# Last layer's attention by query, masks in one pass, and the first modulation in pieces, in a four-layer float32 kernel

## The chip, the cores and the metric

One core of one Trainium2 chip runs the whole program. The metric is the device time of one execution in microseconds; before the change it is 2213.15 (median of 3 runs, 2212.28 to 2214.16). Engines are named as in the profile: PE (TensorE, matrix products), DVE (VectorE), ACT (ScalarE), POOL (GpSimd), SP (SyncE, which issues most transfers).

## The reference

Two blocks of two layers each work on one sequence x of 256 tokens by 1024 features beside a context of 256 tokens. All is float32.

- Each layer: a modulation (six vectors of 1024, from a condition vector times a 1024 x 6144 matrix, for x and for the context), a norm scaled and shifted by it, an input projection, a mixer, an output projection, a second norm and a gated feed-forward of 2816 hidden features.
- Layers 0 and 1 mix by a bidirectional mLSTM, a spatial gating unit and a convolution. Layer 2 mixes by attention, half of its heads with a window of 128 around the query, masked by -1e30. Layer 3, the last, is differential attention, only for the 256 tokens of x:

```
s = einsum('bqhad,bkhad->bhaqk', q, k) * scale        # 8 heads, a = 0, 1, d = 64, 512 keys
p = softmax(s, axis=-1)
a = p[:, :, 0] - lam * p[:, :, 1]
o = einsum('bhqk,bkhe->bqhe', a, v)                    # e = 128
out = (rms(o) * subln * (1 - lam_init)) @ w_out
```

Queries and keys are normed over their 64 features and rotated before that.

## The kernel before

**Layout.** Features lie on partitions, tokens in columns: x and the context together are 512 columns (X and C, 256 each), 8 tiles of 128 features. Every weight product is made of three one-pass products (float32r): high times high, high times low, low times high (`mm3`). The high and low parts of each weight item (1024 rows by 256 columns, 1 MB) are made on the way: ACT rounds (`high_weights`, L2229), DVE subtracts (`low_weights`, L1459), in two halves. Items come through a ring of four slots (`weights` in `sync_program`), SP issues them in order. Attention's own products (scores, logits, sums, transposes) are plain f32.

**Order.** Each engine has its program written out in order, and semaphores (`Signal`) join them. An instruction waits for its counts and all behind it on its engine wait too.

**The start.** SP loads the first third of layer 0's modulation (columns 0 to 2047, shift and scale) as eight steps of 128 rows by 2048 columns into two slots, each step waiting for the product two before it. PE multiplies each with the condition vectors (`mod_step`, 4 products of 512 columns, 32 rows of output each), ACT copies the rows out, PE turns them to columns (`mod_turn`), DVE adds the bias (`bias`) and makes the gains. Only then does `normed` (DVE scales, ACT adds the shift and rounds, DVE makes the low part) feed `first_tiles`: four tiles, products in order of the features as they come (`FIRST`). Meanwhile DVE squares x and the context, POOL adds the squares, PE averages them, ACT makes the root.

**Layer 2's masks.** Windowed scores and logits get their mask as one more product, the identity times `window`, both f32: 16 of 128 columns (`even_scores`) and 8 of 256 (`even_logits`).

**Layer 3.** `odd_projection` makes 24 tiles: per pair of heads two key tiles, two query tiles (256 columns), two value tiles (`ODD_TILES`). Keys and queries are squared by ACT, averaged over heads by PE (`odd_head_sums`), made to roots by ACT, scaled and rotated by DVE (`odd_scaled`, `odd_rotated`, with `odd_swap` on PE). Between tiles PE makes score pairs by query (`odd_scores`: 128 queries, 512 keys, both maps, into banks 2 and 3), and DVE takes only their maxima. After the last tile `odd_mixer` runs 20 steps. Per step, half a head: PE makes the logits anew by key (`odd_logits`, with the maxima subtracted by two products from turned rows), ACT makes the exponentials, PE multiplies both maps with the values (`odd_product`, 512 columns), DVE adds exponentials for the sums of the softmax (`odd_chunks_added`), PE sums them over partitions (`odd_sum`). Per head ACT makes the reciprocal, DVE scales and joins the maps (`odd_joined`), ACT squares, PE averages (`sub_mean`). After every four heads `sub_norm` makes the factors with a square root (another table set of ACT) and a reciprocal. `upper_mixed` multiplies the first four heads' features with the first two output items while the last four wait for their factors; `mixer_out` goes on with the lower features.

Of the kernel before, what the change touches and what calls it, by code (L numbers as in the profile page):

```python
# [13 lines left out]
P = 128  # L14
D = 1024
# [58 lines left out]

THIRD = 2048
SIDES = 2
# [44 lines left out]
class Plan:  # L121
# [54 lines left out]
    def schedule(self):  # L176
# [14 lines left out]
        for s, (place, g) in enumerate(places):  # L191
            self.mod_steps.setdefault(place, []).append(s)
            if s + SIDES < len(places) and s + SIDES >= KD:
                before = g + 6 if g >= 0 else 2
# [8 lines left out]
    def memory(self):  # L203
# [26 lines left out]
        self.decay = sb("state_decay", P, 2, TC, HEADS)  # L230
        self.carried_m, self.minus_end_m = sb("carried_maximum", 64, 5), sb("minus_maximum_at_end", 64, 4)
# [7 lines left out]
        self.odd_rows = at("odd_shift_rows", [P, 4, SEQ], F32R, offset=room)  # L239
# [22 lines left out]
        self.h_low = at("input_low", [P, KD, TOK], F32R, offset=scr_at + (2048 + KD * TOK) * 4)  # L262
        self.bank = [nc.alloc_psum_tensor(f"bank{b}", [P, 512], F32) for b in range(8)]
# [39 lines left out]
        self.od_o, = self.cut(0, (8, SEQ))  # L303
        self.od_PT = big[:, 16:22, :].rearrange("p (b a) n -> p b a n", b=3)
        self.od_rec = big[:, 22, :]
        self.od_pre = [big[:, 23, :], self.rs[:, :]]
        self.sub_sq, self.od_shift = big[:, 0:2, C], big[:, 2, C].rearrange("p (b r) -> p b r", b=2)
        self.sub_ok, self.sub_ms = big[:, 3, C], big[:, 4, C]
        self.od_max, self.od_least = (big[:, 5, SEQ + 8 * q:SEQ + 8 * q + 8].rearrange("p (b j) -> p b j", b=2) for q in range(2))
# [31 lines left out]
    def mod_rows(self, third):  # L341

        return self.scr[:, 0:TOK] if third == 0 else self.rs[:, :]
# [9 lines left out]
    def out_bank(self, L, e):  # L353

        return self.bank[(0, 1, 3, 4)[e % 4] if L == 3 else e % 4]

# [42 lines left out]
    def signals(self):  # L399
        nc = self.nc  # L400

        def S(name, *parts):
# [9 lines left out]
        self.tables_again = S("tables_loaded_again", (0, 7 * 16), (2, 2 * 16))  # L412
        self.stored = nc.alloc_semaphore("stored")
# [4 lines left out]
        self.consts, self.conditions = S("constants_set", (0, 8)), S("conditions_activated", (0, 4))  # L418
        self.params_v, self.lam_exp = S("parameters_derived", (0, 9)), S("lambda_exponents", (0, 2))

        self.stepped, self.mod_out, self.mod_turned = S("modulation_steps_multiplied", (0, 96)), S("modulation_rows_out", (0, 12)), S(
            "modulation_turned", (0, 12))
        self.biased, self.gains = S("modulation_thirds_biased", *((l, 3) for l in layers)), S(
            "norm_gains_made", (0, 4), (1, 4), (2, 5), (3, 4))
# [4 lines left out]
        self.first_squared = S("first_squares_made", *((p, KD) for p in halves))  # L429
        self.squared = S("squares_made", *((p, KD * kinds[p]) for p in order))  # L430
# [58 lines left out]
        self.keys_spread, self.even_set = S("keys_spread", (2, 4)), S("even_constants_set", (0, 4))  # L489
# [8 lines left out]
        self.odd_scores, self.odd_max = S("odd_score_pairs", (0, 16)), S("odd_maxima", (0, 32))  # L498
        self.odd_set, self.odd_shift, self.odd_turned = S("odd_constants_set", (0, 4)), S("odd_shifts", (0, 8)), S("odd_shifts_turned", (0, 4))
        self.odd_high, self.odd_low = S("odd_shifts_high", (0, 4)), S("odd_shifts_low", (0, 8))  # L500
# [2433 lines left out]
```

## Time and profile before

| | |
|---|---|
| runs | 2212.28, 2213.15, 2214.16 us |
| profiled execution | 2211.64 us, span 2209.9 us |
| PE busy | 2106.5 us (95%) |
| DVE busy | 1319.5 us (60%) |
| ACT busy | 996.1 us (45%) |
| POOL busy | 415.4 us (19%) |
| granted PE clock, mean | 0.99 |

The span is the stretch of the profiled execution in which engines work; the execution's own time is 1.7 us longer. PE is the busiest engine; its matmuls are pipelined, so a row's duration holds a latency, and the distance from one start to the next is what an instruction costs in a run of them.

### The profile page before, as it was taken

To read this page: it belongs to the slowest core of one execution; us is meant where nothing else is said; L and a number is where in the kernel's file an instruction comes from. 1 tells how busy PE (TensorE), PEld (TensorE's weight loads), DVE (VectorE), ACT (ScalarE), POOL (GpSimd) and SP (SyncE) were. 2 spreads that over 40 slices of the span, in tenths; PEclk is the share of its full clock that TensorE was granted. 3 is DMA by queue.
4 is the path that set the end of the run, shared out by engine and by line. 5 is a ranking of instruction groups with operands and counts; after the bars stand their busy time and mean duration, and the time that the engine had idled before them with its cause. 6 is when DMAs were issued, how large, how long until landed. Compare 5 with 4: busy or idle time off the path is not lost.

```text
span 2209.9 us, 32689 instructions
## 1 busy us (share of the span) xinstructions
PE 2106.5 (95%) x13156; PEld 1693.0 (77%) x13156; DVE 1319.5 (60%) x2156; ACT 996.1 (45%) x1756; POOL 415.4 (19%) x308
## 2 busy tenths in 40 slices
PE   5999799999999899999999999999999999989999
PEld 2766677978987786999965447797898777648999
DVE  5293757945963666655554345794596555556555
ACT  2434744523542646544553353452354343355443
POOL 1000416502521003000100231650352100000000
PEclk8999999999999999999999999999999999999999
DMA  9654023563466336456533002346344322103563
GB/s 348 205 203 140 20 77 112 185 206 128 172 222 218 120 95 209 135 172 203 179 127 141 1 1 96 132 164 200 109 164 160 126 77 78 56 15 118 170 214 115
DMA packets 264534, 310.07 MB, mean 140 GB/s; under 512 B 5568, under 2 KB 251456, under 8 KB 252096
## 3 DMA queue, kind: packets, MB, share of 16 engines
q1 hardware_dynamic: 259680, 303.33, 41.2%
q10 hardware_dynamic: 4704, 4.65, 0.6%
q8 instruction: 105, 1.72, 0.3%
q14 instruction: 45, 0.37, 0.1%
HBM read 306.91 MB, written 1.05 MB: 139 GB/s over the span
## 4 chain that ended last, share of the span: by engine, by line
PE 80%; DVE 8%; ACT 6%; issue 2%; DMA 2%; POOL 1%; SPq 0%; ACTq 0%; DVEq 0%; POOLq 0%
PE bank L687 79%; DVE weights_low L1465 2%; ACT weights_high L2237 1%; DMA modulation_slots<-w_mod 1%; DVE scratch L1457 1%; DVE big L1457 1%; DVE yT L1457 1%; PE bank L696 1%; DVE big L1953 0%; DVE input_low L1457 0%; DMA modulation_slots<-mod_w 0%; DVE big L2070 0%; DVE token_sums L1813 0%; DVE xT L1457 0%; POOL weight_slots L596 0%
## 5 line engine op out<-in xcount | busy, mean ns | idle before, releaser
L687 PE MATMUL bank<-input_high,weights_high 128*128 128x256 f32 (+1 forms) x2336 | 750.7, 323 | 16.1 <-DVE weights_low L1465 5.4
L687 PE MATMUL bank<-input_high,weights_low 128*128 128x256 f32 (+1 forms) x2336 | 736.2, 317 | 0.0
L687 PE MATMUL bank<-input_low,weights_high 128*128 128x256 f32 (+1 forms) x2336 | 715.0, 317 | 5.7 <-DVE input_low L1457 5.2
L1465 DVE TENSOR_TENSOR weights_low<-weight_slots,weights_high 128x1024 fp32r<-128x1024 f32 (+2 forms) x344 | 391.8, 1178 | 215.4 <-ACT weights_high L2237 214.6
L687 PEld LDWEIGHTS bank<-input_high,weights_high 128*128 128x128 f32 x2336 | 440.4, 189 | 91.8 <-issue 41.2
L687 PEld LDWEIGHTS bank<-input_low,weights_high 128*128 128x128 f32 x2336 | 434.1, 189 | 43.7 <-DVE input_low L1457 10.2
L687 PEld LDWEIGHTS bank<-input_high,weights_low 128*128 128x128 f32 x2336 | 440.2, 188 | 33.7
L2237 ACT ACTIVATE weights_high<-weight_slots 128x1024 fp32r<-128x1024 f32 (+2 forms) x348 | 314.2, 950 | 160.9 <-PE bank L687 147.9
L1808 DVE TENSOR_TENSOR weights_low<-weight_slots,weights_high 128x512 fp32r<-128x512 f32 x216 | 232.0, 1092 | 28.2 <-ACT weights_high L2503 26.1
L687 PE MATMUL bank<-hidden_high,weights_high 128*128 128x256 f32 (+1 forms) x704 | 240.4, 341 | 0.5 <-DVE weights_low L1465 0.4
L687 PE MATMUL bank<-hidden_low,weights_high 128*128 128x256 f32 (+1 forms) x704 | 237.8, 338 | 0.0
L687 PE MATMUL bank<-hidden_high,weights_low 128*128 128x256 f32 (+1 forms) x704 | 237.7, 338 | 0.0
L658 POOL TENSOR_TENSOR yT<-yT 128x256 f32<-128x256 f32 (+1 forms) x66 | 63.4, 965 | 691.4 <-ACT yT L2259 559.1
L1457 DVE SCALAR_TENSOR_TENSOR xT<-bank,modulation,xT 128x256 f32<-128x256 f32 x144 | 64.4, 479 | 208.0 <-PE bank L687 208.0
L687 PEld LDWEIGHTS bank<-hidden_high,weights_high 128*128 128x128 f32 x704 | 132.5, 188 | 30.7 <-issue 8.4
L687 PEld LDWEIGHTS bank<-hidden_high,weights_low 128*128 128x128 f32 x704 | 132.4, 188 | 16.3
L687 PEld LDWEIGHTS bank<-hidden_low,weights_high 128*128 128x128 f32 x704 | 132.5, 188 | 15.4
L2503 ACT ACTIVATE weights_high<-weight_slots 128x512 fp32r<-128x512 f32 x216 | 129.0, 622 | 29.2 <-PE bank L687 14.5
L687 PE MATMUL bank<-modulation_slots,condition_vectors 128*32 128x512 f32 x768 | 103.3, 630 | 25.3 <-DMA modulation_slots<-w_mod 15.6
L687 PE MATMUL bank<-token_sums,weights_high 128*128 128x256 f32 x576 | 105.0, 280 | 3.8 <-ACT scratch L2550 2.6
L687 PE MATMUL bank<-big 64*128 64x256 f32 (+2 forms) x352 | 96.0, 483 | 6.1 <-DVE big L1953 3.0
L591 POOL TENSOR_TENSOR weight_sum<-weight_slots 128x512 f32<-128x512 f32 x36 | 49.2, 1367 | 251.3 <-DVE weights_low L1808 142.7
(284 smaller groups left out, 2678.4 us busy)
## 6 DMA issues: line engine op xcount, KB each, us to landing
modulation_slots<-w_mod SPq DMA_DIRECT2D x48, 1024.0 KB, 7.2
modulation_slots<-mod_w SPq DMA_DIRECT2D x48, 1024.0 KB, 6.7
weight_slots<-w_gu SPq DMA_DIRECT2D x44, 1024.0 KB, 5.1
weight_slots<-ffn_w_in SPq DMA_DIRECT2D x44, 1024.0 KB, 5.1
weight_slots<-w_in SPq DMA_DIRECT2D x24, 1024.0 KB, 5.3
weight_slots<-w_down SPq DMA_DIRECT2D x16, 768.0 KB, 4.8
weight_slots<-ffn_w_out SPq DMA_DIRECT2D x16, 768.0 KB, 4.9
weight_slots<-od_w_in SPq DMA_DIRECT2D x12, 1024.0 KB, 5.1
```

Source lines behind the costliest of these rows:

```text
L591: pool.tensor_tensor(m.weight_sum[:, :, :], a21, a22, ALU.add).then_inc(m.weights_added.sem, 1)
L658: pool.tensor_tensor(o, yT[:, 2 + q, t] if k == 1 else o, yT[:, 2 + i % 4, t], ALU.add).then_inc(m.square_joined.sem, 1)
L687: return pe.matmul(o, w, r, start=start, stop=stop, skip_group_check=shared)
L696: return pe.transpose(o, a, ident[0:a.shape[0], 0:a.shape[0]])
L1457: return stt(out=o, in0=a, scalar=s, in1=b, op0=op0, op1=op1)
L1465: tt(m.w_low[:, g % 2, c], m.ring[:, g % SLOTS, c], m.w_high[:, g % 2, c].bitcast(F32), ALU.subtract).then_inc(m.low_made.sem, 1)
L1808: tt(low, m.raw(run, j), high.bitcast(F32), ALU.subtract).then_inc(m.low_made.sem, 1)
L2237: F(m.w_high[:, g % 2, c], m.ring[:, g % SLOTS, c], ACT.Copy).then_inc(m.high_made.sem, 1)
L2503: F(m.split(j)[0], m.raw(run, j), ACT.Copy).then_inc(m.high_made.sem, 1)
```

## The change

Layer 3:
- The tiles come in another order, keys and queries ahead of values.
- Each of 16 steps x (a head, 128 queries) takes its exponentials from the very scores that gave the maxima: DVE's maxima, times -scale, are ACT's bias; ACT's exponential also sums over the 512 keys. DVE makes both reciprocals, the second times minus lambda; ACT scales the second map (`odd_second`), DVE scales the first and adds (`odd_mix`). PE transposes the joined map in four parts (`odd_flip`), ACT copies it out (`odd_keys`), and one product per head of four 256-column matmuls gives the output (`odd_product`).
- Of these steps 15 start between the projection tiles (`SCORES`, `FLIPS`, `PRODUCTS` give the tile behind which each comes). Logits, picks, turned shifts, the added exponentials and the sums by PE are gone. Head sums use one bank, value tiles two buffers.

Layer 2: the mask and the identity beside it are first copied to float32r, and their products are one-pass.

Start: the first third is loaded as eight pieces of 1024 rows by 256 columns, shift and scale of one pair of feature tiles after the other, into slots of their own. Four are multiplied before the projection, four between its first products. Each pair is copied out, turned, biased and made to gains by itself. The context's squares move from DVE to ACT.

```diff
-ODD_TILES = tuple(8 * part + 2 * i + t for i in range(4) for part in (1, 0, 2) for t in range(2))
+ODD_TILES = tuple(8 * part + 2 * i + t for part, i in ((1, 0), (0, 0), (1, 1), (0, 1), (2, 0), (1, 2), (0, 2), (2, 1), (1, 3), (0, 3), (2, 2), (2, 3)) for t in range(2))
+SCORES = {6: 0, 7: 1, 8: 2, 9: 3, 10: 4, 11: 5, 12: 6, 13: 7, 16: 8, 17: 9, 18: 10, 19: 11, 21: 12, 22: 13, 23: 14, 24: 15}
+FLIPS = {e + 2: x for e, x in SCORES.items()}
+PRODUCTS = {11: 0, 12: 1, 17: 2, 18: 3, 23: 4, 24: 5, 25: 6, 27: 7}
+FIRST_LOADED = tuple((j, k) for k in range(KD - 2) for j in range(2)) + ((0, KD - 2), (0, KD - 1), (1, KD - 2), (1, KD - 1))
+LOADING = {1: ((4,), ()), 2: ((5, 6), ()), 3: ((7,), (2,)), 4: ((), (3,))}
...
@@ sync_program @@
+        if third == 0:
+            at = D * (s % 2) + 256 * (s // 2)
+            sp.dma_start(m.piece(s), w[:, at:at + 256].rearrange("(k p) c -> p k c", p=P)).then_inc(m.loaded(s)[0], 16)
+            return
...
-    for s in range(SIDES):
+    for s in range(4):
         step(s)
     weights(0)
-    for s in range(SIDES, KD):
+    weights(1)
+    for s in range(4, KD):
         step(s)
-    weights(1)
+    weights(2)
...
@@ tensor_program, start @@
+    def first_piece(s):
+
+        i, what = divmod(s, 2)
+        pe.wait_ge(*m.loaded(s))
...
+        for k in range(KD):
+            j = k % 4
+            o = mm(bank[4 + i % 2][32 * j:32 * j + 32, 256 * what:256 * what + 256], m.cvec[:, k, :], m.piece(s)[:, k, :], k < 4, k >= 4)
+        o.then_inc(m.stepped.sem, 1)
+
+    def first_turn(i):
+        pe.wait_ge(*m.mod_out.at(0, i))
+        for c in range(4):
+            o = mm(bank[4 + i % 2][:, 2 * c:2 * c + 2], m.pair_rows(i)[:, c * P:(c + 1) * P], m.summed, True, True)
...
+    pe.wait_ge(*m.consts.at(0, 7))
+    for s in range(3):
+        first_piece(s)
+    pe.wait_ge(*m.columns_in.end(0))
     pe.wait_ge(*m.consts.end(0))
-    for k in range(KD):
-        mod_step(k)
-        if k in (4, 6):
-            add_squares(("first", k // 2 - 2), (X, C)[k // 2 - 2], m.first_squared)
-    pe.wait_ge(*m.columns_in.end(0))
-    mod_turn(0)
+    first_turn(0)
+    first_piece(3)
+    add_squares(("first", 0), X, m.first_squared)
+    add_squares(("first", 1), C)
+    first_turn(1)
     keep_busy(6, 8)
...
@@ tensor_program, layer 2 @@
-                i = mm(bank[2 + half][:, at:at + P], ident[:, :], m.window[:, kind, :], False, True, shared=True)
+                i = mm(bank[2 + half][:, at:at + P], m.unit[:, :], m.mask[:, kind, :], False, True, shared=True)
...
@@ tensor_program, layer 3 @@
+    def odd_flip(x):
+
+        pe.wait_ge(*m.odd_mixed.at(0, x))
+        if x:
+            pe.wait_ge(*m.odd_keyed.at(0, x - 1))
+        for k in range(TC):
+            o = turn(bank[6][:, k * P:(k + 1) * P], m.od_P[:, x % 3, 0, k * P:(k + 1) * P])
+        o.then_inc(m.odd_flipped.sem, 1)
+
+    def odd_product(h):
+        pe.wait_ge(*m.v_tokens.at(3, h | 1 if h < 4 else h))
+        pe.wait_ge(*m.odd_keyed.at(0, 2 * h + 1))
...
+        for k in range(TC):
+            o = mm(m.head_out(h).rearrange("p (c q) -> p c q", c=2), m.od_v[:, h, k, :], m.od_AT[:, h % 2, k, :, :], k == 0, k == TC - 1)
+        o.then_inc(m.odd_prod.sem, 1)
...
         if x:
-            pe.wait_ge(*m.odd_max.at(0, 2 * x - 1))
-        if x and x % 4 == 0:
-            pe.wait_ge(*m.odd_low.at(0, 2 * (x // 4) - 1))
+            pe.wait_ge(*m.odd_exp.at(0, 2 * x - 1))
...
+    def odd_step(e):
+
+        if e in SCORES:
+            odd_scores(SCORES[e])
+        if e in PRODUCTS:
+            odd_product(PRODUCTS[e])
+        if e in FLIPS:
+            odd_flip(FLIPS[e])
...
     def odd_mixer(L):
         odd_projection(L)
         pe.wait_ge(*m.projected.end(L))
         odd_tokens(7)
...
+        odd_step(24)
+        odd_step(25)
+        for u in range(2):
+            sub_spread(u)
+        odd_step(26)
+        for h in (4, 5):
+            sub_mean(h)
+        upper_mixed(L, 0)
+        odd_step(27)
+        sub_mean(6)
+        upper_mixed(L, 1)
+        sub_mean(7)
+        pe.wait_ge(*m.odd_keyed.end(0))
         for u in (2, 3):
             sub_spread(u)
...
@@ vector_program, layer 3 @@
     def odd_maximum(x):
...
+        if x >= 2:
+            dve.wait_ge(*m.odd_exp.at(0, 2 * x - 3))
+        dve.wait_ge(*m.odd_max.at(0, 2 * x + 1))
+        ts(m.od_least[:, x % 2, :], m.od_max[:, x % 2, :], -SCALE, None, ALU.mult).then_inc(m.odd_shift.sem, 1)
...
+    def odd_mix(x):
+        first, second = (m.od_P[:, x % 3, a, :] for a in range(2))
+        dve.wait_ge(*m.odd_second.at(0, x))
+        muladd(first, first, m.od_rec[:, x % 2, 0:1], second).then_inc(m.odd_mixed.sem, 1)
...
+        odd_mix(14)
         to_tokens(L, 7, m.od_v[:, 7, :, :], 4)
...
+        odd_step(24)
+        odd_reciprocals(15)
+        sub_norm(0, range(1, 2))
+        odd_mix(15)
+        odd_step(25)
+        sub_bounded(4)
+        for u in range(2):
+            odd_normalised(u)
+        odd_step(26)
+        sub_bounded(5)
+        next_weights(m.outp[L][0])
...
@@ scalar_program, layer 3 @@
+    def odd_exponential(x):
+
+        act.wait_ge(*m.odd_shift.at(0, x))
...
+        for a in range(2):
+            F(m.od_P[:, x % 3, a, :], bank[2 + a][:, :], ACT.Exp, bias=m.od_least[:, x % 2, a:a + 1], scale=SCALE,
+              accum_out=m.od_den[:, x % 2, a:a + 1]).then_inc(m.odd_exp.sem, 1)
+
+    def odd_second(x):
+        second = m.od_P[:, x % 3, 1, :]
+        act.wait_ge(*m.odd_rec.at(0, 2 * x + 1))
+        F(second, second, ACT.Identity, scale=m.od_rec[:, x % 2, 1:2]).then_inc(m.odd_second.sem, 1)
+
+    def odd_step(e):
+        if e in FLIPS:
+            odd_keys(FLIPS[e])
+        if e in SCORES:
+            odd_exponential(SCORES[e])
+            odd_second(SCORES[e])
...
@@ scalar_program, start @@
     ln_exp_tables()
+    pair_out(0)
+    act.wait_ge(m.inputs_in[1], 16)
+    for k in range(KD):
+        square(("first", 1), k, C)
+    pair_out(1)
+    high_weights(0)
     act.wait_ge(*m.square_added.end(("first", 0)))
     act.wait_ge(*m.square_added.end(("first", 1)))
     rstd("first", slice(0, TOK))
-    high_weights(0)
-    modulate("start", KD - 1)
```

## Rows read from the trace of the kernel before

**Rows 1.** The page, busy us (share) by engine, and the chain that ended last.

```profile
PE 2106.5 (95%) x13156; PEld 1693.0 (77%) x13156; DVE 1319.5 (60%) x2156; ACT 996.1 (45%) x1756; POOL 415.4 (19%) x308
...
PE 80%; DVE 8%; ACT 6%; issue 2%; DMA 2%; POOL 1%; SPq 0%; ACTq 0%; DVEq 0%; POOLq 0%
```

**Rows 2.** Windows of the last layer: stretch, busy us by engine, PEclk, DMA share, GB/s.

```profile
1771.00:1911.00 140.00, 135.41 (x653) 100.74 (x653) 73.50 (x125) 56.99 (x96) 0.00 (x0) 1.00 0.26 83
1911.00:1981.00 70.00, 69.68 (x293) 33.04 (x290) 40.46 (x75) 33.83 (x63) 0.00 (x0) 1.00 0.00 1
1981.00:1987.00 6.00, 0.03 (x1) 0.00 (x0) 3.73 (x5) 3.35 (x6) 0.00 (x0) 0.70 0.11 19
1987.00:1990.00 3.00, 2.93 (x11) 2.12 (x12) 1.33 (x5) 1.41 (x2) 0.00 (x0) 0.50 0.92 316
```

**Rows 3.** Timeline of the start: start us, us, engine, line, operation, [idle before].

```profile
22.48 5.43 DVE L2204 TENSOR_TENSOR yT<-xT 128x256 f32<-128x256 f32 x8 [2.94 <-DMA xT<-p_ctx]
...
35.11 0.69 ACT L2284 ACTIVATE rstd<-bank,eps 128x512 f32<-128x512 f32 x1 [22.99 <-PE bank L687]
...
36.69 1.06 PE L687 MATMUL bank<-modulation_slots,condition_vectors 128*32 128x512 f32 x8 [1.67 <-DMA modulation_slots<-w_mod]
...
38.98 1.03 PE L687 MATMUL bank<-ident,scratch 128*128 128x8 f32 x8 [1.23 <-ACT scratch L2252]
...
42.36 0.76 PE L687 MATMUL bank<-input_high,weights_high 128*128 128x512 f32 x1
...
66.14 0.39 PE L687 MATMUL bank<-input_high,weights_high 128*128 128x512 f32 x1
...
66.37 0.40 PE L687 MATMUL bank<-input_low,weights_high 128*128 128x512 f32 x1
```

**Rows 4.** One window of the start, columns as in group 2.

```profile
50.00:55.00 5.00, 5.00 (x23) 3.99 (x22) 5.00 (x14) 3.31 (x7) 0.00 (x0) 1.00 1.10 349
```

**Rows 5.** DMA issues of the first 60 us: KB each, median us to landing.

```profile
xT<-p_x ACTq DMA_DIRECT2D x1, 1024.0 KB, 12.9
```

**Rows 6.** Groups of instructions: out<-in, forms, count, busy us, mean ns.

```profile
L687 PE MATMUL bank<-tables,ident 128*128 128x128 f32 (+1 forms) x48 | 10.5, 343 | 0.0
```

**Rows 7.** Timeline between two projection tiles of the last layer.

```profile
1806.52 1.02 PE L687 MATMUL bank<-scratch,mean_over_head_halves 128*128 128x512 f32 x2
...
1807.21 2.00 ACT L2237 ACTIVATE weights_high<-weight_slots 128x1024 fp32r<-128x1024 f32 x2
...
1811.00 0.75 DVE L1457 SCALAR_TENSOR_TENSOR big<-big,parameter_columns,scratch 128x512 f32<-128x512 f32 x1 [7.23 <-ACT scratch L2728]
...
1811.67 1.28 DVE L2070 TENSOR_REDUCE big<-bank 128x1 f32<-128x512 f32 x2
...
1812.87 2.35 DVE L1465 TENSOR_TENSOR weights_low<-weight_slots,weights_high 128x1024 fp32r<-128x1024 f32 x2
...
1813.00 1.13 PE L687 MATMUL bank<-big 64*128 64x512 f32 x4
```

**Rows 8.** Timeline of the last layer's attention, from tile 23 to the output projection.

```profile
1910.84 0.60 PE L696 MATMUL bank<-ident,big 128*128 128x128 f32 x4
...
1913.45 1.14 PE L687 MATMUL bank<-big 64*128 64x256 f32 x8
...
1914.86 1.08 ACT L2757 ACTIVATE big<-bank 128x512 f32<-128x512 f32 x2 [3.22 <-PE bank L687]
...
1918.22 1.98 PE L687 MATMUL bank<-big,yT 128*128 128x512 f32 x4
...
1986.70 1.28 ACT L2775 ACT_TABLE_LOAD   x1
...
1987.07 1.06 PE L687 MATMUL bank<-big,mean_over_d 128*32 128x256 f32 x2 [6.04 <-DVE big L2112]
...
1989.73 1.75 DVE L2126 RECIPROCAL big<-big 128x256 f32<-128x256 f32 x1 [0.48 <-ACT big L2775]
...
1997.35 0.36 PE L687 MATMUL bank<-input_high,weights_high 128*128 128x256 f32 x1 [0.71 <-DVE input_low L2138]
```

More of the change, by code:

```diff
@@ L739, in keep_busy, with loading, first_tiles @@
             mm(bank[b][:, 0:P], m.mean_d[:, :], ident[:, :], True, True)
-    def first_tiles(items, n, place, part, last):
-        for j, k in FIRST:
+    def loading(k):
+        pieces, turns = LOADING.get(k, ((), ()))
+        for s in pieces:
+            first_piece(s)
+        for i in turns:
+            first_turn(i)
+    def first_tiles(items, n, place, part, last, first=False):
+        for j, k in FIRST_LOADED if first else FIRST:
+            if first and j == 0:
+                loading(k)
             if k in (0, KD // 2):
@@ L1373, in odd_projection @@
         odd_head_sums(1)
-        pe.wait_ge(*m.odd_set.end(0))
         for e in range(4, 24):
@@ L1486, in modulate, with first_pair @@
             bias(m.mod_turn[place])
+    def first_pair(i):
+        r = slice(2 * i, 2 * i + 2)
+        dve.wait_ge(*m.mod_turned.at(0, i))
+        o = m.mods[:, 0, :, 0:16].rearrange("p v (s k) -> p s k v", s=2)[:, :, r, :]
+        b = cols[:, L_TAB[0], B_MOD:B_MOD + 16].rearrange("p (s k) -> p s k", s=2)[:, :, r].unsqueeze(3).to_broadcast([P, 2, 2, 2])
+        tt(o, bank[4 + i % 2][:, 0:8].rearrange("p (s k v) -> p s k v", s=2, k=2), b, ALU.add).then_inc(m.biased.sem, 1)
+        dve.wait_ge(*m.biased.at(0, i))
+        for v in range(2):
+            muladd(m.coef[:, 0, v, r], m.mods[:, 0, v, 8 + 2 * i:10 + 2 * i], 1.0, column(L_TAB[0], N1 + 2 * i, 2), ALU.add,
+                   ALU.mult).then_inc(m.gains.sem, 1)
     def gains(l4, which):
         at, s = ((N1, 8), (N2, 32))[which]
-        dve.wait_ge(*m.biased.at(l4, 2 * which))
+        dve.wait_ge(*m.biased.at(0, m.third_at(3 * l4 + 2 * which)))
         for v in range(2):
@@ L1511, in normed @@
             t = slice(v * SEQ, (v + 1) * SEQ)
+            if L == 0 and which == 0 and i % (2 * per) == 0:
+                if k >= 2:
+                    for j in range(made, i):
+                        low(j)
+                    made = i
+                    first_pair(k // 2)
+                dve.wait_ge(*m.gains.at(0, k + 1))
             if k >= 2:
@@ L2297, in normed @@
             t = slice(v * SEQ, (v + 1) * SEQ)
+            if L == 0 and which == 0 and i == 4 * per:
+                pair_out(2)
+                pair_out(3)
             act.wait_ge(*m.norm_t.at(part, i))
@@ L2737, in odd_projection @@
             n = SEQ if tile < 8 else TOK
-            projected_tile(L, e, ACT.Copy, big[:, tile, 0:n], n, banks=2)
+            if tile >= 18:
+                act.wait_ge(*m.v_turned.at(L, tile - 18))
+            projected_tile(L, e, ACT.Copy, big[:, tile if tile < 16 else 16 + tile % 2, 0:n], n, banks=2)
             coming_weights(L, e)
```

446 lines of the change are left out of this document (187 added, 259 removed).

## The prediction

> **What bounds the kernel now.** The page comes first: PE is busy 95% of the span, and the chain that ended last is 80% PE, 8% DVE, 6% ACT [rows 1]. A change therefore gains where it takes PE work away or closes one of PE's few gaps. The windows of the last layer come next [rows 2]: while its tiles are projected (1771 to 1911) PE is busy 135.4 of 140 us at full clock, DVE only 73.5 and ACT 57.0; in the attention that follows (1911 to 1981) PE is busy 69.7 of 70, DVE 40.5 and ACT 33.8; then PE stands still for 6 us, and after it the granted clock is 0.50 (1.2 GHz). So PE is the limit of the attention and has no room; DVE and ACT have some 65 and 80 us of room under the projections. The start is another matter: there transfers and a chain of small steps hold the first projection back to 42.36 [rows 3, 4].
>
> **The last layer, PE work.** From the transposes after the next to last tile's products (1910.84, about the end of tile 23) to the first product of the output projection's lower half (1997.35) the kernel takes 86.5 us [rows 8]. PE's f32 costs: 512 columns over 128 rows take 0.43 each of two instructions, 0.85 a product (head sum, 1.02 with its latency [rows 7]); four instructions of 512 take 1.7 (1.98 with latency, [rows 8]); the pair of scores on 64 rows each 0.96 (1.13 with latency, [rows 7]); four transposes 0.5 (0.60). Gone are 16 logits (eight instructions of 256 columns, 0.8 [rows 8], and two picks, 0.5: 21 us), 16 halves of products (1.7 each: 27), 8 sums (0.85: 7), 4 turns of shifts (0.65: 3): 58 us. New are 16 flips (0.5: 8) and 8 products of four 256-column matmuls, 8 instructions at 0.21 (1.7: 14): 22 us. The 16 score pairs stay and now carry the exponentials. PE work falls by 36 us, but much of the rest moves under the projections, and PE is full there.
> Until tile 23 is done PE now has two more score pairs (14 instead of 12: 1.9), 12 flips (6), four products (6.8), four sub-norm sums (2), less three turns (2): +14.7.
>
> **The last layer, the new loop.** Each scored step now chains both other engines. From a tile's end ACT copies it out (0.5), in every second step cuts weights (2.0), squares (0.5) and makes the root (1.35); DVE scales (0.7) and begins the maxima 5.15 us after the tile's end (1806.52 to 1811.67 [rows 7]), and ends them at 6.4. New behind them: shift 0.2, a gap 0.2, two exponentials 1.3 (1.08 as now [rows 8], and 0.1 each for reading their sums), at 8.1; then reciprocal, product with lambda and the second map's scaling 1.5 (the scaling is a 128x512 pass of ACT like an exponential, about 0.6; two small DVE steps and gaps are the rest), at 9.6. Only then is ACT free for the next tile. In even steps DVE first mixes the last maps (0.7, as the scaling of that size, 0.75), then splits weights (2.35), scales and takes maxima: 8.2 to 8.9 from one exponential to the next. PE in the same time has its tile (24 matmuls at 0.233 [rows 3] or, for the 256 columns of queries, half of it: 5.6 or 2.8), head sum, swap, scores, flip and in some steps a product: 7.5 to 8.1 in key and value steps, but 4.7 to 7.4 in query steps. PE's next scores wait for the last exponentials (they share the banks). Going through the steps in order, the waits are 1.1 and 1.2 at scores 1 and 2, 1.3 and 2.1 at 6 and 7, 0.8 and 2.1 at 10 and 11, 0.5 at 12 (queries late in rotation); value steps without scores let the loop catch up. Sum 9.1. Waits of today in that stretch, for maxima and shifts, go: 3.8 of the 4.6 us idle. Queued behind ACT's long step are the copies out, which free PE's two banks; a copy late by up to 2 us is still ahead of the tile after the next. Tile 23 thus ends 14.7 + 9.1 - 3.8 = 20.0 later. Bounds: no waits at all, +11; every step at the loop's length with nothing caught up, +32.
>
> **The last layer, the tail.** Count from the end of tile 23. Scores 14 at 0.5, exponentials to 4.6, scores 15 to 5.7, product 5, flip 13, product 6, flip 14 to 10.9. DVE meanwhile mixes map 14, copies the last values and takes maxima 15 (to 9.4), ACT's exponentials end at 11.2, its scaling at 12.7; then a table load 1.28, the root, and DVE's reciprocal 1.75 [rows 8]: factors at 16.8. PE idles 6 us, spreads, flips map 15 (mixed only behind the factors) and idles 3.7 more until the first four heads are scaled, cut and head 5's squares are summed (24.1). Upper output tiles of 24 matmuls (2.8) to 26.9; product 7 to 28.6; copy, square, bound, and the second upper tiles beside them to 31.9; the last sum to 32.4. Now comes the end chain with nothing beside it: bounds, root, reciprocal, factor 4.0, spread, scale and cut 2.7 (today's chain from 1987.07 holds the same steps around its 24 + 24 upper products [rows 8]): 39.2. After each of the three long gaps I expect half clock for about 3 us as in the window from 1987 [rows 2], 4 us in all: 43.2. Against 86.5 that is -43.3. Together: 20.0 - 43.3 = **-23.3**, range -34 to -8.
>
> Today's rows have transposes four at a time between long products, at full clock [rows 2, 8]; the change adds 64. The Trainium skill (TensorE: Matmul & The Clock Gate, Part 4: PE-mode transpose) says that transposes don't count as busy for the clock as other matmuls do, which speaks against them. By the rows they cost 8 us in all and the sum stands; by that rule the clock could fall around them, which is rival 3.
>
> **The masks of the layer before.** The 24 window masks are f32 products with the identity, 48 instructions, 10.5 us busy [rows 6]. As one-pass products they are 24 instructions of at most the 0.117 that a one-pass product of 256 columns takes: 2.8. They stand in chains of PE itself (scores, maxima, next scores; logits, exponentials), so most of the 7.7 us shows: I take **-6**, range -7.7 to -3. Two small DVE copies (under 0.5 us) are issued before its first weights, where today two picks of 1.4 us in all cost nothing.
>
> **The start.** Today ctx lands at 22.5, the last of eight modulation transfers shortly before 36.69, each held by two slots; root, weights, turn (1.03), gains and first scaling bring the first product to 42.36; the 96 products of the first four tiles (22.4 at 0.233, as 66.14 to 66.37, and 1.4 for the second weights and half clock) end at 66.14 [rows 3]. The new order needs four of the eight pieces, x, ctx and two weights before it begins: 1.05 MB each, 8.9 MB with the small tables; in 1 KB rows the engines move 350 GB/s (349 in the window from 50, when the weights' 1 KB rows are under way [rows 4]). From 2.4 us that is 28, with weights 0 there at about 25. ACT's cuts (2.0), the root (1.3), first scaling and high part (1.5) give a start at 30.5. But then PE carries four pieces (1.06 each [rows 3]) and two turns (1.0 each) inside: 22.4 + 6.3 = 28.7, and 2.3 for the second weights and the low clock: 61.5, which is **-4.6**. The later pieces land at 31, 34, 37, 40, each a little ahead of its place; DVE's three pair steps (0.7 each) fit, since DVE needs 4.8 us for two k and PE 5.6 and more. Bounds: start at 28 and nothing late, -8.5; ctx late (below), +2.
> What sets ctx: x needed 12.9 us for 1 MB beside modulation rows of 8 KB [rows 5], and ctx came at 22.5 [rows 3]. If the queues share as today, it comes at 24 to 26, and its squares on ACT (8 of about 0.5) end at 28 to 30; that is the +2. The Trainium skill (DMA: Bandwidth & Descriptors, Queues, rings and completion order) says that each engine alternates between queues packet by packet; with 1 KB rows on both sides ctx would then come sooner, near 15. The sum would stay as it is, since weights 0 set the start then, and the worse end would fall away; the row of x agrees so far that the queue with the small rows got a quarter of the bytes.
>
> **Sum.** -23.3 - 6 - 4.6 = -33.9. The profiled execution took 2211.64 (span 2209.9), the runs' median is 2213.15, 1.5 more. 2211.64 - 33.9 = 2177.7, and with the 1.5: **2179 us**.
>
> **Rivals.**
> (1) The loop binds more than I count (a wait of mine is missing, as the single bank for head sums, or copies out late enough to hold tiles): every scored step at the loop's length, +12 in the projections: 2191. For it: 8.7 us loops against 4.7 us steps; against: the value steps give slack back.
> (2) The loop binds less and the tail overlaps better (clock not falling in it): -9: 2170. For it: DVE and ACT have 65 and 80 us of room [rows 2].
> (3) Slower: the clock. If waits of 1 to 2 us in each step, with flips between, let the granted clock fall to 0.50 under the projections, PE's some 150 us of work there double where it is low. The gain is gone once 34 us of this work run at half clock; with half of the 150 low it is 2179 + 75 = 2254. Against it: waits of up to 1.4 us in the kernel before left the clock at 1.00 over 140 us [rows 2].
> (4) The part at the start gives nothing or costs 2, since ctx and the turns come late: 2184 to 2186, within the forecast's range.
>
> **Chances.** Forecast with (4) (2171 to 2189) 0.58; (1) 0.17; (2) 0.12; (3) 0.07; something between that eats up most of the gain 0.06, half of it within 0.2% of before (about what can be told from no change). Faster 0.89, same 0.03, slower 0.08. The range of 8 in 10 reaches into (1) and (2): 2162 to 2206.
>
> **What would show it.** First product of the kernel at 29 to 33 and tile 4 at 60 to 63; fewer than 3 us of mask products; no logits, no picks; PE waits for exponentials at scores 1, 2, 6, 7, 10 and 11 of 1 to 2 us; tile 23 about 20 us later from the layer's start and its tail 39 to 47 us long, with two gaps of over 3 us and one before the last spreads. Wrong would be: a granted clock under 1.00 in the projections, waits of over 15 us there, a tail over 55 us, or a first tile group that ends no sooner than today.

## The result: 17 us faster, half of what was forecast

| | median of runs, us | lowest to highest | against before |
|---|---|---|---|
| before | 2213.53 | 2212.28 to 2214.16 (4) | 1 |
| after | 2195.82 | 2194.65 to 2200.44 (4) | 0.9923 [0.9911, 0.9936] |

The change makes the kernel faster by 0.77%. The forecast was 2179 with a range of 2162 to 2206: the time lies in the range, the gain (17.7 by the medians, 17.0 by the ratio) is half of the 34 forecast. The profiled executions took 2211.64 and 2194.65, 16.99 apart, and that difference can be divided. From the page of after, the two lines that [rows 1] shows of before:

```profile
PE 2079.4 (95%) x13092; PEld 1694.3 (77%) x13092; DVE 1306.3 (60%) x2173; ACT 1014.0 (46%) x1811; POOL 414.4 (19%) x308
...
PE 78%; DVE 9%; ACT 7%; issue 3%; DMA 1%; POOL 1%; ACTq 0%; SPq 0%; DVEq 0%; POOLq 0%
```

PE is busy 27.1 us less, and only 17 come out: 10 went into idle time. To find the places I took four instructions that stand in both kernels and set their starts beside each other: the first product of layer 2 (1105.72 before, 1101.69 after), the first product of layer 3 (1756.10, 1752.96), the transposes behind tile 23 (1910.84, 1931.76) and the first lower-half output product (1997.35, 1980.33). The stretch from layer 3's first product to the end of tile 23 is called the loop below, the one from there to the lower-half product the tail.

| stretch | before | after | difference | forecast |
|---|---|---|---|---|
| start to layer 2 | 1105.7 | 1101.7 | -4.0 | -4.6 |
| layer 2 to layer 3 | 650.4 | 651.3 | +0.9 | -6 |
| layer 3 to the end of tile 23 | 154.7 | 178.8 | +24.1 | +20.0 |
| tail | 86.5 | 48.6 | -37.9 | -43.3 |
| rest of the span | 212.6 | 212.7 | +0.1 | 0 |

The start did what was forecast. Of after, the timeline at the context's squares, at the first product and at the fifth tile (before's are in [rows 3]):

```profile
19.36 1.34 ACT L2314 ACTIVATE yT<-xT 128x256 f32<-128x256 f32 x4 [4.11 <-DMA xT<-p_ctx]
...
30.99 0.47 PE L722 MATMUL bank<-input_high,weights_high 128*128 128x512 f32 x1 [0.37 <-ACT input_high L2362]
...
61.21 0.47 PE L722 MATMUL bank<-input_high,weights_high 128*128 128x512 f32 x1 [0.62 <-DVE weights_low L1507]
```

First product at 30.99 (forecast 30.5), fifth tile at 61.21 (61.5), where it was 66.14. The context is used from 19.36 on, neither as late as the 24 to 26 that I had worked out from today's sharing of the queues nor as soon as 15. By the start of layer 2 what is gained can't be read from two profiles: in the three profiled kernels with the old start (before, masks_only, layer3_only) layer 2 begins at 1105.7 to 1108.9, in the nine with the new one at 1100.9 to 1110.2; their fifth tiles begin at 66.1 to 69.0 and 61.2 to 62.6.

The loop of layer 3 is where a wait was missing from the forecast. The waits of PE in after from layer 3's first product to its output projection (total, times, longest):

```profile
PE bank L722 <- DVE modulation_slots L2157: 18.2, 4, 8.2
PE bank L722 <- DVE big L2186: 4.0, 1, 4.0
PE bank L722 <- DVE xT L2162: 2.4, 1, 2.4
PE bank L722 <- ACT big L2809: 2.4, 4, 1.6
```

Line 2157 is DVE's copy of a head's product out of its bank (`odd_joined`). Four waits for it are 18.2 us: 3.93 and 4.07 in the loop, 1.94 and 8.23 in the tail. The waits that I had placed in the loop, at scores for exponentials (9.1 us), are the last row, and there only 0.8 us of it; 1.6 is in the tail. Around the first of the four, the timeline of after says why:

```profile
1840.68 0.75 DVE L1499 SCALAR_TENSOR_TENSOR big<-big 128x512 f32<-128x512 f32 x1 [0.79 <-ACT big L2815]
1841.35 2.35 DVE L1507 TENSOR_TENSOR weights_low<-weight_slots,weights_high 128x1024 fp32r<-128x1024 f32 x2
1843.62 0.74 DVE L1499 SCALAR_TENSOR_TENSOR big<-big,parameter_columns,scratch 128x512 f32<-128x512 f32 x1
1844.29 0.41 DVE L2157 COPY modulation_slots<-bank 128x256 f32<-128x256 f32 x1
1844.85 0.45 PE L722 MATMUL bank<-modulation_slots,yT 128*128 128x256 f32 x1 [3.93 <-DVE modulation_slots L2157]
```

Product 0 was done at 1835.3. DVE mixes a map, cuts the next weights and scales a tile before it copies, and product 1, one step later, uses the same bank.

The longest of the four is in the tail, where DVE makes the factors (the reciprocal and the product behind it) and mixes map 15 before it copies product 5, and product 6 waits for that copy:

```profile
1949.62 1.75 DVE L2184 RECIPROCAL big<-big 128x256 f32<-128x256 f32 x1 [2.52 <-ACT big L2850]
1951.41 0.43 DVE L2186 TENSOR_TENSOR big<-big 128x256 f32<-128x256 f32 x1
1951.75 0.75 DVE L1499 SCALAR_TENSOR_TENSOR big<-big 128x512 f32<-128x512 f32 x1
1952.41 0.42 DVE L2157 COPY modulation_slots<-bank 128x256 f32<-128x256 f32 x1
1952.97 1.62 PE L722 MATMUL bank<-modulation_slots,yT 128*128 128x256 f32 x3 [8.23 <-DVE modulation_slots L2157]
```

The clock is the other part. Windows of after: layer 2's attention, the loop, and four stretches of the tail (columns as in [rows 2]):

```profile
1207.00:1222.00 15.00, 13.62 (x45) 6.70 (x46) 4.53 (x8) 3.06 (x6) 0.00 (x0) 0.53 0.00 1
```

```profile
1773.00:1932.00 159.00, 148.88 (x713) 110.66 (x713) 90.11 (x183) 88.03 (x172) 0.00 (x0) 0.98 0.22 73
1932.00:1941.00 9.00, 5.47 (x29) 3.26 (x28) 5.30 (x13) 3.25 (x7) 0.00 (x0) 1.00 0.00 0
1941.00:1953.00 12.00, 3.77 (x13) 2.77 (x13) 4.59 (x9) 5.64 (x9) 0.00 (x0) 0.67 0.00 0
1953.00:1963.00 10.00, 7.91 (x26) 6.00 (x26) 3.98 (x11) 3.40 (x9) 0.00 (x0) 0.71 0.01 2
1963.00:1981.00 18.00, 13.75 (x73) 10.76 (x74) 8.86 (x17) 5.03 (x8) 0.00 (x0) 0.85 0.18 58
```

In layer 2's attention PE had 0.53, so nearly all of that window was at 1.2 GHz; the granted clock there was low for 17.1 us in one piece, before for 3.4. PE had idled 1.2, 0.3 and 1.8 us just ahead, in both kernels (1.1 for the first in before). In the loop it was low for 3.4 us behind each of the two 4 us waits, hence 0.98; in the tail it was low for 3.4, 10.2 and 6.8 us.

### The profile page after: what moved, and what is told of

Its sections match the earlier page's. It is cut to its first block, busy times and chain, and to the rows that moved or that the text cites. A ratio compares the mean times of both kernels' runs of the same rounds, so it can differ in the third digit from the quotient of the medians.

```text
span 2193.0 us, 32660 instructions
## 1 busy us (share of the span) xinstructions
PE 2079.4 (95%) x13092; PEld 1694.3 (77%) x13092; DVE 1306.3 (60%) x2173; ACT 1014.0 (46%) x1811; POOL 414.4 (19%) x308
## 4 chain that ended last, share of the span: by engine, by line
PE 78%; DVE 9%; ACT 7%; issue 3%; DMA 1%; POOL 1%; ACTq 0%; SPq 0%; DVEq 0%; POOLq 0%
PE bank L722 78%; DVE weights_low L1507 2%; ACT weights_high L2292 1%; DVE scratch L1499 1%; PE bank L731 1%; DMA parameter_columns<-p_columns 1%; DVE big L1499 1%; DVE yT L1499 1%; DVE big L2017 0%; DVE input_low L1499 0%; ACT big L2809 0%; DVE xT L1499 0%; DMA modulation_slots<-w_mod 0%; DMA modulation_slots<-mod_w 0%; DVE token_sums L1877 0%
## 5 line engine op out<-in xcount | busy, mean ns | idle before, releaser
L1872 DVE TENSOR_TENSOR weights_low<-weight_slots,weights_high 128x512 fp32r<-128x512 f32 x216 | 231.9, 1092 | 27.8 <-ACT weights_high L2566 25.9
L2566 ACT ACTIVATE weights_high<-weight_slots 128x512 fp32r<-128x512 f32 x216 | 129.0, 623 | 29.2 <-PE bank L722 14.5
L722 PE MATMUL bank<-modulation_slots,condition_vectors 128*32 128x512 f32 (+1 forms) x768 | 96.3, 598 | 13.9 <-DMA modulation_slots<-w_mod 11.0
L2314 ACT ACTIVATE yT<-xT 128x256 f32<-128x256 f32 (+1 forms) x64 | 32.8, 521 | 151.0 <-DVE xT L1499 145.8
```

Of the source, the lines that this page charges most:

```text
L722: return pe.matmul(o, w, r, start=start, stop=stop, skip_group_check=shared)
L1872: tt(low, m.raw(run, j), high.bitcast(F32), ALU.subtract).then_inc(m.low_made.sem, 1)
L2314: F(yT[:, 2 + k % 4, t], xT[:, k, t], ACT.Square).then_inc(m.squared.sem, 1)
L2566: F(m.split(j)[0], m.raw(run, j), ACT.Copy).then_inc(m.high_made.sem, 1)
```

## Experiments

Each was timed in turn with the kernel before, and has its ratio to it; in runs that scattered more than the ones above (single executions of the kernel before from 2208.4 to 2220.1). They were made in three groups, each with runs of before of its own (medians 2212.91, 2212.47 and 2212.27), so kernels are compared with each other by their ratios. Where I give a difference in the trace, it is between one profiled execution of each.

**Each part alone.** Three kernels take the kernel before with one part of the change.

```
masks_only:   the lines with m.unit, m.mask, even_set
start_only:   first_piece, first_turn, first_pair, pair_out, FIRST_LOADED and their counts
layer3_only:  everything with odd_, sub_, SCORES, FLIPS, PRODUCTS
```

> The kernel before with one part of the change alone: layer 2's masks and the identity beside them are copied to float32r and their products are one-pass. Theory A (from the trace after: layer 2's attention ends as late as before against its start, and the granted clock is 0.50 for about 17 us at its beginning, where it was low for about 3): the 7.7 us of mask products go and the longer half clock takes them back, 0 to -2 us against before. Rival B (my prediction's step): the clock in the trace after comes from another part of the change, and the masks alone bring -6 (range -7.7 to -3).

> The kernel before with the new start alone (first third in eight pieces, context squares on ACT). Theory A: the 4.9 us by which the fifth tile starts sooner in the trace after reach the end, -4.9 (-4 to -6). Rival B: the shifted start also shifts where the granted clock falls later, and part of it goes, -1 to -3.

> The kernel before with layer 3's part alone. In the trace after, tile 23 ends 25.9 us later from the layer's start and the tail is 37.9 us shorter (48.6 against 86.5). Theory A: the part stands by itself, -12 us (-10 to -14). Rival B (my prediction): -23, and the other parts disturbed it.

| | median, us | ratio |
|---|---|---|
| before | 2212.91 | |
| masks_only | 2210.35 | 0.9990 [0.9978, 1.0002] |
| start_only | 2209.25 | 0.9985 [0.9971, 0.9998] |
| layer3_only | 2200.98 | 0.9944 [0.9925, 0.9962] |

That is -2.2, -3.3 and -12.4 us by the ratios, -17.9 in all: the parts add up to the change, as far as their intervals (each some 5 to 8 us wide) can tell. Layer 3's part alone has its -12 (A holds, my -23 does not); in its trace the loop takes 179.7 us and the tail 48.6, as in after. (By the starts above, tile 23 ends 24.1 us later in after, not the 25.9 of the expectation.) For the start the interval reaches from -6.4 to -0.4 and holds both theories. For the masks the timing can't tell -2 from nothing; the trace can. From layer 2's first product (1107.63) to the first product behind its attention (1315.26), layer 2's stretch below, masks_only takes 207.6 us, before 212.0, after 212.9. Both before and masks_only have 3.4 us of low clock there. So the masks alone are worth **-4.3** (the rival's reason, within its range; A's long stretch did not come with them here), and the 17.1 us of after cost 5.2 more than those 3.4. The size was mine to get right: in masks_only a pair of scores' masks holds PE from 1220.86 to 1221.23, before from 1220.57 to 1221.21:

```profile
1220.86 0.44 PE L689 MATMUL bank<-window_mask,mask_unit 128*128 128x128 f32 x2
1221.23 0.69 PE L689 MATMUL bank<-big 64*128 64x512 f32 x1
```

```profile
1220.57 0.71 PE L687 MATMUL bank<-tables,ident 128*128 128x128 f32 x4
1221.21 0.69 PE L687 MATMUL bank<-big 64*128 64x512 f32 x1
```

That is 0.27 saved eight times and, by the same comparison at the logits (1.06 against 0.43), 0.63 four times: 4.7, not 7.7. The old masks cost 9.4 us by their starts where I had taken 10.5 of busy time, which holds each group's latency; the new ones cost 4.7 where I had put down 2.8, since a pair of one-pass products takes 0.37 or 0.43 and not twice 0.117. The second is the larger error.

**The copy first in its step.**

```diff
@@ vector_program, odd_projection of the kernel after @@
         for e in range(24):
+            if e - 1 in PRODUCTS:
+                odd_joined(PRODUCTS[e - 1])
             if e - 1 in SCORES:
                 odd_mix(SCORES[e - 1])
...
-            odd_step(e)
+            odd_step(e, False)
```

> The changed kernel with one order changed: in layer 3's projection loop DVE copies a head's product out first in its step, ahead of the mixing, the cut of the weights and the scaling. Theory A: the two waits of PE of 3.93 and 4.07 us (products 1 and 3, which share the bank of the product before) stem from that queue alone; they shrink below 0.8 each, the two stretches of 3.4 us at half clock behind them go as well: -7 to -10 us against the kernel after. Rival B: the loop of ACT and DVE binds anyway and PE waits at the next scores instead: 0 to -3.

2188.3, ratio 0.9879 [0.9860, 0.9898], against 0.9923 for after: -9.7 us by the ratios. Its waits of PE, from layer 3's first product to the end of tile 23, and the window of the loop:

```profile
PE bank L722 <- ACT big L2811: 1.4, 4, 0.4
PE bank L722 <- ACT scratch L2791: 1.2, 2, 1.0
PE bank L722 <- DVE rstd L2124: 1.0, 3, 0.6
```

```profile
1767.00:1927.00 160.00, 156.17 (x773) 116.21 (x771) 95.46 (x193) 94.67 (x184) 0.00 (x0) 1.00 0.22 73
```

Around product 1, where after waited 3.93 us:

```profile
1844.51 0.42 DVE L2157 COPY modulation_slots<-bank 128x256 f32<-128x256 f32 x1
...
1845.55 1.99 PE L722 MATMUL bank<-modulation_slots,yT 128*128 128x256 f32 x8
```

No row for the copy is left, the clock is 1.00, and tile 23 ends 168.7 us after layer 3's first product instead of 178.8: -10.1. Of that 8.0 is the two waits; 6.8 us at half clock are worth at most 3.4, less 0.6 us of waits that came at the scores instead, which is about the rest. A holds, in the time too: the intervals of after and join_first lie apart.

The other traces say the same of the clock. Four kernels have the two waits (after, layer3_only, no_masks, warm_masks), and behind each of these eight waits of 3.9 to 4.1 us the granted clock was low for 3.4 or 6.8 us. In the other eight kernels the longest wait in the loop is 1.0 or 1.4 us, and the loop has no low clock.

**Masks undone, and a warm PE.**

```diff
@@ no_masks: even_scores (and even_logits alike) of the kernel after @@
-                i = mm(bank[2 + half][:, at:at + P], m.unit[:, :], m.mask[:, kind, :], False, True, shared=True)
+                i = mm(bank[2 + half][:, at:at + P], ident[:, :], m.window[:, kind, :], False, True, shared=True)
@@ warm_masks: even_projection, even_mixer of the kernel after @@
+                if e == 12:
+                    pe.wait_ge(*m.projected.at(L, 10))
+                    keep_busy(0, 5)
                 even_scores(0, e - 7)
...
+        keep_busy(0, 7)
         even_turn(0)
```

> The changed kernel with layer 2's masks as they were before (f32 products of the identity), the rest changed. Layer 2's attention, from the first wait of PE behind its last tile to the next projection tile of 24 products, took 110.24 us before, 106.61 with the masks alone and 111.83 in the kernel after, where the granted clock is 0.50 for 17.1 us in it (3.4 in the others). Theory A (the masks save 3.6 us, and the longer half clock, which comes with the masks at this place in time, takes them and 1.6 more): 110.2 here with 3.4 us low, and a whole time 0 to 2 us shorter than the kernel after. Rival B (the long half clock comes from the new start, whatever the masks): a stretch of 17 us here too, 115 us, and 3 to 5 us slower than the kernel after.

> The changed kernel with products that nothing reads in two waits of PE in layer 2 (5 of 128 columns ahead of the last but one pair of scores of the first group, where PE waits 1.23 us for DVE, 7 ahead of the first turned shifts, where it waits 1.76). Theory A (the clock falls because PE idles there): the stretch at half clock shrinks from 17.1 to 3.4 us or nothing, the attention takes 106 to 107 us instead of 111.83, the whole is 4 to 6 us shorter. Rival B (the clock falls for the kind of work, products of 64 rows and of one pass): the stretch stays, and the time too or +0.5.

no_masks: 2198.89, ratio 0.9940 [0.9924, 0.9956]; its attention has 3.4 us at the low clock and layer 2's stretch takes 212.1 us. Its trace looks as A has it; in time it is no shorter than after (+3.8 by the ratios, the intervals overlap). The 3.8 is near what the masks save in masks_only (4.3), as it would be if most executions of after had no long stretch; that isn't shown. warm_masks: ratio 0.9926 [0.9908, 0.9944], median 2192.95 of five executions; a sixth took 8343.16 us and is left out (with it the median is 2196.74). Its window over the same time as after's above:

```profile
1207.00:1222.00 15.00, 12.57 (x71) 6.35 (x69) 7.49 (x15) 3.33 (x6) 2.34 (x1) 1.00 0.00 1
```

The clock stays at 1.00 and layer 2's stretch takes 206.7 us, 6.2 less than after. This one profile fits A, that the idling lets the clock fall and not the kind of product. It doesn't show it: in best, which has the same products in the same gaps, the clock was low for 3.4 us a little later, and the ratio of warm_masks' runs is about that of after (0.9923). What the six kernels with one-pass masks and without these extra products had in that place was 3.4 us of low clock in three (masks_only, exp_first, tail), 10.2 in one (tail_two) and 17.1 in two (after, join_first), with the same instructions and the same waits of PE ahead of it; the four with f32 masks had 3.4. One profile each: whether the shorter masks make a long stretch more likely stays open.

**Exponentials ahead of the copy of the turned map.**

```diff
@@ scalar_program, odd_step, on top of join_first @@
-        if e in FLIPS:
-            odd_keys(FLIPS[e])
         if e in SCORES:
             odd_exponential(SCORES[e])
+        if e in FLIPS:
+            odd_keys(FLIPS[e])
+        if e in SCORES:
             odd_second(SCORES[e])
```

> The kernel with DVE's copy first in its step (run join_first), and besides in each step ACT makes the exponentials of the newest scores ahead of copying the turned map out; before it waited there for PE's turn of an older map, which stands behind a product. Theory A: in the projections little is left to gain (PE idles 4 us in all from 1770 to 1925), but in the tail exponentials 14 and 15 start 1.6 and 3 us sooner, which the roots, factors and spreads behind them inherit: -4 to -5 us against join_first. Rival B: the copy of the turned map comes later and holds PE's products and turns instead: 0 to -1.

2184.02, ratio 0.9869 [0.9854, 0.9884]: -2.2 by the ratios, less than the 4 to 5 expected, and with intervals that overlap the runs alone don't show a gain. The trace holds both theories: the first factors come 15.8 us behind tile 23 instead of 20.1 in after, and the tail is 45.2 us instead of 48.6 (-3.4); but the loop takes 170.2 instead of 168.7, with two new waits of 0.5 us of PE's turns for that copy. The swap belongs in the tail alone (not tried).

**The tail in another order.**

```diff
@@ tensor_program, odd_mixer @@
         odd_step(26)
+        odd_step(27)
-        for h in (4, 5):
+        for h in (4, 5, 6):
             sub_mean(h)
         upper_mixed(L, 0)
-        odd_step(27)
-        sub_mean(6)
+        sub_mean(7)
         upper_mixed(L, 1)
-        sub_mean(7)
@@ vector_program, odd_mixer @@
-        to_tokens(L, 7, m.od_v[:, 7, :, :], 4)
-        odd_step(24)
+        odd_maximum(15)
+        to_tokens(L, 7, m.od_v[:, 7, :, :], 4)
+        odd_joined(4)
+        odd_joined(5)
         odd_reciprocals(15)
+        next_weights(m.outp[L][0])
         sub_norm(0, range(1, 2))
...
```

The lines left out order the rest of DVE's tail, and ACT's, to match: the cut of the next weights first, the squares of heads 4 and 5 ahead of the cuts of the scaled heads.

> exp_first with the tail in another order: DVE copies products 4 and 5 out ahead of the reciprocals, so product 6 no longer waits behind the factors (8.2 us of wait in the kernel after); the cut of the next weights goes into the gaps of both engines before the factors; product 7 comes ahead of the first upper output tiles instead of behind them. Theory A (the tail is one chain, exponentials 15, root, factors, turn 15, product 7, square, mean, root, factors, and the order only put other work into it): from the end of tile 23 to the first lower-half output product 35 to 38 us instead of 48.6, -7 to -8 us against exp_first. Rival B (the granted clock at 0.50 in the long idle takes it back): -3.

2176.79, ratio 0.9831 [0.9817, 0.9846]; the tail takes 36.1 us, -8.4 against exp_first by the ratios and -9.1 in the trace. A holds. Product 6 waits 0.7 us where it waited 6.7 in exp_first, but product 5 now waits 3.4 for the copy of product 4. Several moves were made at once, and no run tells what each is worth.

```diff
@@ tail_two, tensor_program, odd_mixer @@
-        for h in (4, 5, 6):
+        for h in (4, 5, 6, 7):
             sub_mean(h)
         upper_mixed(L, 0)
-        sub_mean(7)
@@ tail_two, vector_program: odd_joined(4) ahead of odd_reciprocals(14), then @@
-        odd_mix(14)
         odd_maximum(15)
+        odd_mix(14)
+        odd_joined(5)
         to_tokens(L, 7, m.od_v[:, 7, :, :], 4)
-        odd_joined(4)
-        odd_joined(5)
         odd_reciprocals(15)
@@ best: tail_two with warm_masks' lines, and in tensor_program, odd_mixer @@
+        keep_busy(0, 8)
         for u in range(2):
             sub_spread(u)
```

> Run tail with four more moves in the same stretch: product 4 is copied out ahead of the reciprocals of step 14, the maxima of step 15 come ahead of the mixing of map 14, the reciprocals of step 15 wait for no product any more, and the last mean over head 7's squares comes ahead of the first upper output tiles. Theory A (the tail is one chain; what an engine has queued ahead of its links is the rest of the loss): the first factors are ready 4 to 5 us sooner, the second 1.9 sooner; from the end of tile 23 to the first lower-half product 29 to 31 us instead of 36.1; -5 to -7 against tail. Rival B (PE's own work there, scores 15, products 5 and 6, two turned maps, sets the pace, above all if its clock is low): 33 to 34, -2 to -3.

> tail_two with products that nothing reads in three waits of PE: two in layer 2's attention as in run warm_masks (5 and 7 of 128 columns), one ahead of the first spreads in layer 3's tail (8). Theory A: layer 2's attention takes 105.7 us as in warm_masks (106.7 in tail), and no stretch at half clock follows the first spreads: -2 to -4 against tail_two, or more where that one falls into a long stretch at half clock. Rival B: the waits they fill are shorter now and the products stand in the way: 0 to +1.

tail_two: 2167.0, ratio 0.9812 [0.9788, 0.9835], -4.2 against tail with intervals that overlap. In the trace product 5 waits no more, the first spreads come 4.9 us sooner from tile 23's end than in tail, and the tail takes 30.95 us, 5.1 less: A in the trace, not told apart by the time. The two spreads of its tail, where after has them 25.6 and 45.0 us behind tile 23 (here 14.3, at 1934.66, and 28.35, at 1948.71):

```profile
1934.66 2.90 PE L722 MATMUL bank<-big,ident 128*128 128x256 f32 x8 [2.19 <-DVE big L2184]
...
1948.71 1.89 PE L722 MATMUL bank<-big,ident 128*128 128x256 f32 x8
```

best: 2167.57, ratio 0.9795 [0.9778, 0.9812]. Its tail takes 29.6 us, 1.4 less, at full clock throughout, but layer 2's stretch takes 208.3 (3.4 us at the low clock) and not the 206.7 of warm_masks, so half of A failed; against tail_two the medians are equal and the intervals overlap. Both are faster than after by 24 us (0.9812 against 0.9923) or more, and about as fast as each other.

## Why the forecast was right in direction and off by half

- **What bounds the kernel**: right. PE's busy time fell by 27 us, and what came out was decided by its idle time and clock in three places.
- **The start, -4.6**: right, for the reasons given (30.99 and 61.21 against 30.5 and 61.5). Of the 4.9 us at the fifth tile 4.0 are left at layer 2, where profiles of equal starts differ by 3 to 9 us; what reaches the end is only known as -3.3, between -6.4 and -0.4.
- **The masks, -6**: -4.3 with the clock as it was (masks_only), inside its range of -7.7 to -3; the one-pass products, put at 2.8 us, cost 4.7. The term also missed the stretch at half clock, which cost 5.2 in the profiled execution and turned it into +0.9. How often an execution has it isn't known, so how much of the 5.2 us is bad luck stays open. The clock was in my list of rivals for layer 3 alone; that PE already idled 1.8 us in this attention, at its low stretch of before, I had not looked at.
- **The loop, +20.0**: measured +24.1. The work term (14.7) holds: join_first, with 3.6 us of waits (the three rows above), ends tile 23 14.0 us later than before, and 14.7 + 3.6 - 3.8 is 14.5. The waits term was wrong in its place: 9.1 at scores, measured 0.8. An exponential ends 4 to 8 us behind the start of its scores, but PE's own steps between scores took 7.4 to 8.1 us and only once 5.9 (join_first), where I had put down 4.7 to 7.4 for those with queries. What I had left out is the wait of a product for the copy of the one before. I had not asked what is queued ahead of `odd_joined` on DVE: 8.0 us in two places, and 3.4 us of half clock behind each. **This is the failed step**: the overlap of products that share a bank, put at nothing. That the loop came out only 4.1 us off is luck, as the 8.3 us too many at the scores all but cancel the 8.0 too few at the copies. Rival (1) named its kind ("a wait of mine is missing") and its bank wrongly; its 2191 is nearer to the time than my 2179, but its 12 us in the loop were not there.
- **The tail, -43.3**: measured -37.9. I had product 6 and flip 14 done at 10.9; product 6 began at 21.2, since product 5 stood in its bank until DVE copied it, which DVE does only behind the first factors: the same failed step, a wait of 8.2 us, then at half clock. The factors themselves came at 20.1 instead of 16.8, as ACT copied a turned map ahead of exponentials 14 and 15 (with that order changed they come at 15.8, exp_first). So the first spreads are 8.8 us late (25.6 for 16.8): 3.3 by the factors, 5.5 by product 6 and flip 14 between them and the spreads. The rest of the chain had about the right length: 12.9 us from the first upper output tile to the last spreads (32.1 to 45.0) where I had 12.3 (24.1 to 36.4). The 4 us that I had allowed for the clock hide part of the miss.
- **Rival (3), the clock**: not as forecast, but alive in small. The 64 transposes did nothing to it: join_first has 1.00 over 160 us that hold 12 of the 16 turned maps. By the rule of the Trainium skill (TensorE: Matmul & The Clock Gate, Part 4: PE-mode transpose) the clock might have fallen around them; between full-size products this case doesn't show it. What the clock fell behind were the waits of 4 us and, in layer 2, the three of 1.2, 0.3 and 1.8 us. Of the signs that I had named for being wrong one came, a granted clock under 1.00 in the projections (0.98). Of those for being right the masks' 3 us (4.7), the waits for exponentials of 1 to 2 us (0.8 in all in the loop) and the tail's 39 to 47 us (48.6) failed.
- **The sum**: the errors are +6.9 in layer 2 (1.7 the size of the masks, 5.2 the low clock), +4.1 in the loop, +5.4 in the tail and +0.6 at the start. The 9.5 of layer 3 come back in layer3_only, and most of them trace to the copies of the products, the order of ACT in the tail and the clock behind the waits.

## What to carry to other kernels

When two products use one bank in turn, the copy between them is on PE's path: find it in the other engine's order, add up what stands ahead of it, and move it to the front of its step. Here one moved line was worth 10 us, and the same look at the tail, with several moves on three engines, another 15. In a chain over three engines, what an engine has queued ahead of a link costs as much as the link. Where PE waits about 4 us among its products, price the next 3 to 7 us at half clock too, as behind all eight such waits here. Take what short instructions cost, old and new, from the distance between starts, not from their busy time or from a longer product's share.

## What the runs showed of the hardware

- The granted clock fell to 0.50 behind each of eight waits of PE of 3.9 to 4.1 us (for 3.4 or 6.8 us) and, in all ten profiles without extra products in layer 2, within 7 us of the last of three idle times there (1.1 or 1.2, 0.3 and 1.8 us, close together). Behind a single 1.8 us near the start of layer 2 (from 1138.36 in before) it fell in one of the twelve (join_first).
- Products that nothing reads, put into two of layer 2's gaps, went with a clock of 1.00 in one profile (warm_masks: layer 2's stretch 206.7 us instead of 212.9) and with 3.4 us of low clock in another (best: 208.3).
- The same instructions with the same waits had 3.4, 10.2 or 17.1 us of low clock in layer 2, in six profiles of kernels that don't differ there: a difference of 5 us for which no line of layer 2 stands.
- The context, in a queue beside 1 KB rows, landed 14.4 us after its issue and was used at 19.36. The Trainium skill (DMA: Bandwidth & Descriptors, Queues, rings and completion order) has the queues served in turn packet by packet; worked out from that I had near 15 for its arrival, and from the trace before 24 to 26. Neither holds; the sum did not depend on it.
